# Trunk kernel with a routed expert layer: expert steps of 1024, slabs of 2048, tokens fetched by an indexed DMA

## What is computed

```python
def swiglu(h, w_gate_up, w_down):
    gt, up = jnp.split(h @ w_gate_up, 2, axis=-1)
    return (jax.nn.silu(gt) * up) @ w_down

def moe_swiglu(h, w_router, w_gate_up, w_down):
    t = h.reshape(-1, dm)
    top_val, top_idx = lax.top_k((t @ w_router).astype(jnp.float32), TOP_K)
    top_w = jax.nn.softmax(top_val, axis=-1)
    combine = jnp.sum(jax.nn.one_hot(top_idx, N_EXPERTS) * top_w[..., None], axis=1)
    y = jnp.zeros_like(t)
    for e in range(N_EXPERTS):
        y = y + combine[:, e:e + 1] * swiglu(t, w_gate_up[e], w_down[e])
```

## Time and profile before

| what | value |
|---|---|
| median of 3 runs | 1815.71 us (1814.45 to 1817.58) |
| profiled execution, span from first to last instruction | 1814.0 us |
| expert loop: first matmul of slot 0 | at 793.56 us |
| one slot, steady | 126.2 us, 575 matmul records |
| PE busy over the span | 1770.4 us (98%) |
| DVE, ACT busy over the span | 1375.4 us (76%), 1179.4 us (65%) |
| DMA over one slot | 349 GB/s |

### The profile page before, as it was taken

The page is one execution under the profiler, slowest core; times in us unless marked ns, Lnnn a source line. Parts: engine busy times, 40 slices in busy tenths (PEclk is TensorE's granted clock), DMA queues, the critical chain, the costliest instruction groups (busy, mean ns, idle before and its releaser), DMA issues.

```text
span 1814.0 us, 25521 instructions
## 1 busy us (share of the span) xinstructions
PE 1770.4 (98%) x8224; PEld 1431.1 (79%) x8224; DVE 1375.4 (76%) x1336; ACT 1179.4 (65%) x1313; POOL 79.9 (4%) x108
## 2 busy tenths in 40 slices
PE   7999999999999999889999999999999999999998
PEld 5777877888887778668888888888888888888886
DVE  5654665555665566578998998989989988989987
ACT  5557454434555655357777777777777778777775
POOL 4210000000112100000000000000000000000000
PEclk9999999999999999979999999999999999999999
DMA  8544545656564444749999999999999999999991
GB/s 269 163 142 136 172 142 177 188 182 192 167 196 140 145 149 152 276 174 348 370 335 351 358 342 347 351 345 356 337 349 364 334 353 361 334 356 362 335 352 66
DMA packets 214408, 479.15 MB, mean 264 GB/s; under 512 B 18224, under 2 KB 20304, under 8 KB 214352
## 3 DMA queue, kind: packets, MB, share of 16 engines
q1 hardware_dynamic: 212640, 474.18, 75.6%
q0 software_dynamic: 1712, 4.24, 0.8%
HBM read 477.31 MB, written 1.05 MB: 264 GB/s over the span
## 4 chain that ended last, share of the span: by engine, by line
PE 92%; DVE 4%; ACT 1%; POOL 1%; issue 1%; DMA 0%; DVEq 0%; POOLq 0%; ACTq 0%
PE pa L1663 22%; PE pa L1664 22%; PE pa L1665 22%; PE ps L1663 6%; PE ps L1765 6%; PE ps L1665 6%; PE ps L1664 6%; PE pa L2045 1%; POOL hrs L642 1%; PE ps L1627 1%; DVE w_lo L1094 1%; PE ps L1759 0%; ACT scr L964 0%; DMA gain<-in_mem_norm_g 0%; DVE xt L1130 0%
## 5 line engine op out<-in xcount | busy, mean ns | idle before, releaser
L1663 PE MATMUL pa<-w_hi,r 128*128 128x512 f32 x1496 | 601.4, 402 | 3.0 <-DVE w_lo L1552 3.0
L1665 PE MATMUL pa<-w_hi,r 128*128 128x512 f32 x1496 | 591.3, 395 | 0.0
L1664 PE MATMUL pa<-w_lo,r 128*128 128x512 f32 x1496 | 591.0, 395 | 0.0
L1094 DVE TENSOR_TENSOR w_lo<-w_raw,w_hi 128x1024 fp32r<-128x1024 f32 (+2 forms) x229 | 277.5, 1227 | 140.7 <-ACT w_hi L746 132.9
L746 ACT ACTIVATE w_hi<-w_raw 128x1024 fp32r<-128x1024 f32 (+2 forms) x229 | 237.3, 1050 | 178.6 <-PE pa L1665 154.4
L1663 PEld LDWEIGHTS pa<-w_hi,r 128*128 128x128 f32 x1496 | 281.7, 188 | 69.2 <-DVE w_lo L1552 3.2
L1665 PEld LDWEIGHTS pa<-w_hi,r 128*128 128x128 f32 x1496 | 281.4, 188 | 67.0
L1664 PEld LDWEIGHTS pa<-w_lo,r 128*128 128x128 f32 x1496 | 281.9, 188 | 62.8
L1552 DVE TENSOR_TENSOR w_lo<-w_raw,w_hi 128x1024 fp32r<-128x1024 f32 x160 | 192.3, 1223 | 19.5 <-ACT w_hi L1032 17.1
L1032 ACT ACTIVATE w_hi<-w_raw 128x1024 fp32r<-128x1024 f32 x160 | 167.9, 1060 | 37.9 <-PE pa L1665 21.7
L1663 PE MATMUL ps<-w_hi,r 128*128 128x512 f32 x448 | 177.7, 397 | 0.0
(11 more groups left out here) (261 smaller groups left out, 2041.9 us busy)
## 6 DMA issues: line engine op xcount, KB each, us to landing
w_raw<-in_w_in SPq DMA_DIRECT2D x104, 512.0 KB, 4.3
w_raw<-in_moe_w_gate_up SPq DMA_DIRECT2D x96, 512.0 KB, 5.2
scr<-in_moe_w_gate_up SPq DMA_DIRECT2D x88, 512.0 KB, 5.3
w_raw<-in_moe_w_down SPq DMA_DIRECT2D x64, 512.0 KB, 5.1
w_raw<-in_ff_w_gate_up SPq DMA_DIRECT2D x44, 512.0 KB, 4.5
gates<-in_moe_w_down SPq DMA_DIRECT2D x40, 512.0 KB, 5.1
scr<-in_moe_w_down SPq DMA_DIRECT2D x40, 512.0 KB, 4.8
gr<-in_moe_w_gate_up SPq DMA_DIRECT2D x32, 512.0 KB, 5.4
```

Of the source, the lines that this page charges most:

```text
L1094: dve.tensor_tensor(w_lo[:, s % SPLIT, 0:w], raw_slot(s)[:, 0:w], w_hi[:, s % SPLIT, 0:w].bitcast(F32), ALU.subtract)\
L1663: pe.matmul(dst, hi, m_hi, start=first, stop=False)
L1664: pe.matmul(dst, hi, m_lo, start=False, stop=False)
L1665: return pe.matmul(dst, lo, m_hi, start=False, stop=last)
```

## The change

All SBUF tiles of the trunk and of the expert part are laid out anew, so that the expert part has large tiles of its own over the trunk's. In the expert part:

- Steps are 1024, 1024, 1024 and 512 hidden columns wide, so there are 4 in place of 7.
- A slab is 128 x 2048 (1 MB, 12 matmuls), so a slot has 42 in place of 84. There are 14 raw places in place of 21, and a ring of 3 split slabs in place of 4, with 2 splits ahead of each block in place of 3.
- ACT copies the turned hidden columns first and takes the silu second, since there is now one tile `hs` for both.
- The tokens of slots 1 and on are no longer gathered by `sel`. Two matmuls with two columns (`find_tokens`) give each place its token's number, DVE writes it as an integer (`token_of`), POOL fetches the rows from a copy of the tokens in DRAM (`h_rows`) by an indexed DMA into `xg_tok`, and PE turns them in 8 transposes. `xg` is split by ACT and DVE after that.
- For slot 0 the tokens are gathered by 16 matmuls in plain float32 in place of 32 in fp32r.
- Slot 0 stands outside the loop. It has no scatter, and DVE makes most of the slot tables inside it (`slot_tables`), after its first gate block. Two splits of ACT and DVE come ahead of the gather.

The raw places lie over tiles of the trunk. Eight of the 14 can be loaded at once after the last merge (13 of 21 before); two more wait for the trunk's last split, one for the last norm, two for the router's matmuls, and one for the first gather and the copy of the tokens to DRAM.

```diff
-EXP_RAW, EXP_SPLIT = 21, 4
-EXP_AHEAD = EXP_SPLIT - 1
+EXP_SLAB = 2048
+EXP_RAW, EXP_RING = 14, 3
+EXP_AHEAD = EXP_RING - 1
...
-STEPS = D_EXP // BW
-HT = BW // P
-GU = KT * BW // SLAB
-EXP_SLABS = STEPS * (2 * GU + HT)
-assert EXP_SLABS % EXP_RAW == 0 and EXP_SLABS % EXP_SPLIT == 0
+STEP = [(c, min(DM, D_EXP - c)) for c in range(0, D_EXP, DM)]
+STEPS = len(STEP)
+GU = [KT * w // EXP_SLAB for _, w in STEP]
+DN = [w // P * DM // EXP_SLAB for _, w in STEP]
+EXP_SLABS = sum(2 * a + b for a, b in zip(GU, DN))
+HT = DM // P
+HT_END = STEP[-1][1] // P
+assert EXP_SLABS % EXP_RAW == 0 and EXP_SLABS % EXP_RING == 0
...
+        exp_raw_a = sb("exp_raw_a", [P, 10, EXP_SLAB])
+        hs = sb("hs", [P, DM])
+        exp_hi = sb("exp_hi", [P, EXP_RING, EXP_SLAB], F32R)
+        exp_lo = sb("exp_lo", [P, EXP_RING, EXP_SLAB], F32R)
+        sb("under_gain", [P, DM])
+        exp_raw_b = sb("exp_raw_b", [P, 4, EXP_SLAB])
...
+        exp_slots = [exp_raw_a[:, n, :] for n in range(7)] + [exp_raw_b[:, 3, :]] \
+            + [exp_raw_a[:, n, :] for n in (8, 9, 7)] + [exp_raw_b[:, n, :] for n in (1, 2, 0)]
+        W_RAW_SLOT, GATES_SLOT, XT_SLOT, HN_SLOT = 8, 10, 11, 13
...
+                    if j == XT_SLOT:
+                        sp.wait_ge(slab_used, PRE)
+                    if j == HN_SLOT:
+                        sp.wait_ge(gathered, 1)
+                        sp.wait_ge(h_stored, 16)
+                    dst = exp_slots[j % EXP_RAW].rearrange("p (k n) -> p k n", k=n)
+                    sp.dma_start(dst, src).then_inc(more_ready[j % EXP_RAW], 16)
...
+            pool.wait_ge(norm_done, NT * 3 * LAYERS)
+            pool.dma_start(h_rows[:, :].rearrange("(t p) d -> p t d", p=P), hn[:, :, :])\
+                .then_inc(h_stored, 16)
+            pool.wait_ge(h_stored, 16)
+            def fetch_tokens(i):
+                pool.wait_ge(token_ready, i + 1)
+                pool.sem_inc(token_seen, 1)
+                pool.indirect_dma_start(
+                    out=xg_tok[:, :], out_offset=None, in_=h_rows[:, :],
+                    in_offset=bass.IndirectOffsetOnAxis(ap=token_of[:, 0:1], axis=0),
+                    bounds_check=SEQ - 1, oob_is_err=False).then_inc(token_loaded, 16)
+            fetch_tokens(0)
+            pool.wait_ge(r_table, 1)
+            slots = pool.value_load(slot_i[0:1, 0:1], min_val=EXPERTS, max_val=SLOTS)
+            with pool.Fori(1, slots) as i:
+                fetch_tokens(i)
...
+                def silu(s):
+                    w = STEP[s][1]
+                    act.wait_ge(slab_used, at + (PRE + used))
+                    act.activation(hs[:, 0:w], pa[:, 0:w], ACT.Silu).then_inc(e_silu, 1)
+                def hidden_hi(s):
+                    act.wait_ge(e_turned, i * STEPS + (s + 1))
+                    dst, src = (hts, ps[:, DM:2 * DM]) if s < STEPS - 1 else \
+                        (hts_end, pa[:, BW:2 * BW])
+                    act.activation(dst[:, 0, :, :].rearrange("p k c -> p (k c)"), src, ACT.Copy)\
+                        .then_inc(e_hi, 1)
+                if type(i) is not int:
+                    expert_split(i, EXP_AHEAD)
+                    act.wait_ge(slab_used, at + PRE)
+                    act.activation(ysp[:, 0, :], ps[:, 0:DM], ACT.Copy).then_inc(y_hi, 1)
+                for s in range(STEPS):
+                    uses(GU[s])
+                    if s > 0:
+                        hidden_hi(s - 1)
+                    silu(s)
+                    uses(GU[s])
+                    if s == 0:
+                        act.wait_ge(selt_turned, i + 1)
+                        act.activation(selT[:, :], ps[:, DM:DM + SEQ], ACT.Copy)\
+                            .then_inc(selt_ready, 1)
+                    elif s < STEPS - 1:
+                        uses(DN[s - 1])
+                uses(DN[STEPS - 2] // 2)
+                tokens_hi(i + 2)
+                hidden_hi(STEPS - 1)
+                uses(DN[STEPS - 2] // 2)
+                uses(DN[STEPS - 1])
+                j = 0
...
+            expert_split(0, 1)
...
+            expert_split(0, EXP_AHEAD)
+            def tokens_lo(n):
+                dve.wait_ge(xg_hi, n)
+                dve.tensor_tensor(xg[:, 1, :, :].rearrange("p k c -> p (k c)"), ps[:, DM:2 * DM],
+                                  xg[:, 0, :, :].rearrange("p k c -> p (k c)").bitcast(F32),
+                                  ALU.subtract).then_inc(xg_lo, 1)
+            tokens_lo(1)
...
+            def slot_tables():
+                dve.sem_inc(added, NT)
+                link(dve.memset(ozero, 0.0))
+                link(dve.memset(slot_comb, 0.0))
...
+                if type(i) is not int:
+                    expert_split(i, EXP_AHEAD)
+                    output_lo(i)
+                for s in range(STEPS):
+                    uses(GU[s])
                     if s > 0:
+                        hidden_lo(s - 1)
+                    elif type(i) is int:
+                        slot_tables()
                     else:
                         add_slot(i)
+                    uses(GU[s])
+                    hidden(s)
+                    if s == 0:
                         dve.wait_ge(selt_turned, i + 1)
                         for t in range(NT):
                             dve.tensor_scalar(sel[:, t, :], iota_c[:, :],
                                               slot_pos[:, t, bass.ds(i + 1, 1)], None,
                                               ALU.is_equal).then_inc(sel_ready, 1)
+                    elif s == 1:
+                        dve.wait_ge(token_found, i + 1)
+                        dve.tensor_copy(token_of[:, :], ps[:, DM:DM + 1]).then_inc(token_ready, 1)
+                    if 0 < s < STEPS - 1:
+                        uses(DN[s - 1])
+                uses(DN[STEPS - 2] // 2)
+                tokens_lo(i + 2)
+                hidden_lo(STEPS - 1)
+                uses(DN[STEPS - 2] // 2)
+                uses(DN[STEPS - 1])
+                j = 0
+            expert(0)
...
+            def find_tokens(n):
+                pe.wait_ge(sel_ready, (n + 1) * NT)
+                for t in range(NT):
+                    ins = mm(ps[:, DM:DM + 2], sel[:, t, :], token_no[:, t, :], t == 0, t == NT - 1)
+                ins.then_inc(token_found, 1)
...
+            pe.wait_ge(sel_ready, NT)
+            for k in range(KT):
+                for t in range(NT):
+                    ins = mm(ps[:, DM + k * P:DM + (k + 1) * P], hn[:, t, k * P:(k + 1) * P],
+                             sel[:, t, :], k % 4 == 0 and t == 0, t == NT - 1)
+            ins.then_inc(gathered, 1)
...
+                pe.wait_ge(xg_hi, i + 1)
+                pe.wait_ge(xg_lo, i + 1)
+                for s in range(STEPS):
+                    if s > 0:
+                        pe.wait_ge(e_silu, i * STEPS + s)
+                    block(0, s)
+                    if s > 0:
+                        if s == 1:
+                            pe.wait_ge(selt_ready, i + 1)
+                        elif s == 2:
+                            pe.wait_ge(token_ready, i + 1)
+                        turn_hidden(s - 1)
+                    elif type(i) is not int:
+                        scatter(i)
+                    block(1, s)
+                    if s == 0:
+                        if type(i) is not int:
+                            pe.wait_ge(added, i * NT + NT)
+                        for t in range(NT):
+                            ins = pe.transpose(ps[:, DM + t * P:DM + (t + 1) * P], sel[:, t, :],
+                                               ident[:, :])
+                        ins.then_inc(selt_turned, 1)
+                    elif s < STEPS - 1:
+                        if s == 1:
+                            pe.wait_ge(e_lo, i * STEPS + 1)
+                            find_tokens(i + 1)
+                        down(s - 1, range(DN[s - 1]))
+                half = DN[STEPS - 2] // 2
+                down(STEPS - 2, range(half))
+                pe.wait_ge(token_loaded, i * 16 + 16)
+                for k in range(KT):
+                    ins = pe.transpose(ps[:, DM + k * P:DM + (k + 1) * P],
+                                       xg_tok[:, k * P:(k + 1) * P], ident[:, :])
+                ins.then_inc(gathered, 1)
+                turn_hidden(STEPS - 1)
+                down(STEPS - 2, range(half, 2 * half))
+                down(STEPS - 1, range(DN[STEPS - 1]))
```

More of the change, by code:

```diff
@@ L1006, in _, with expert_split @@
             act.wait_ge(slab_used, PRE)
-            for t in range(NT):
-                act.activation(th[:, 0, t, :], hn[:, t, :], ACT.Copy).then_inc(r_hi, 1)
+            j = 0
+            def expert_split(i, n):
+                nonlocal j
+                while j < min(n, EXP_SLABS):
+                    act.wait_ge(more_ready[j % EXP_RAW], i * (16 * EXP_SLABS // EXP_RAW)
+                                + 16 * (j // EXP_RAW + 1))
+                    act.wait_ge(slab_used, i * EXP_SLABS + (PRE + j - EXP_RING + 1))
```

(31 more changed lines are left out.)

442 lines of the change are left out of this document (172 added, 270 removed).

## The result

| what | before | after |
|---|---|---|
| median | 1816.45 us (1814.45 to 1817.58, 4 runs) | 1785.91 us (1785.56 to 1788.15, 4 runs) |
| ratio | 1 | 0.9835, 95% interval 0.9821 to 0.9849 |
| span of the profiled execution | 1814.0 us | 1784.0 us |
| one slot, steady | 126.23 us | 123.67 us (forecast 125.9) |

The changed kernel is 1.65% faster. The forecast was 1814.4 us with a range of 1803 to 1824, so it was wrong by 28.5 us, and the time lies outside the range.

What follows compares the result with a forecast made beforehand. PE, busy 98% and never waiting in the expert loop, was taken as the bound. Terms -17.3 - 1.8 + 14.8 - 0.7 + 3.7 = -1.3 us gave a span of 1812.7 and a median of 1814.4 us, range 1803 to 1824.

Steps and rivals of the forecast that it cites:

- the first line of the sum: PE's work in a slot: 504 matmuls stay, at 0.2333 us each, 117.6 of the slot's 126.2 us.
- PE's list: PE's instructions in a slot: half gathers go, token transposes and find_tokens come, net -2.16 us a slot, -17.3 for 8.
- Waits at the gate blocks' ends: Steps 1, 2, 3: PE waits 0.76, 0.76 and 0.33 us for the next split, +14.8 us for 8 slots.
- the chain: Gate block's end: ACT's copy, silu and split, then DVE's split, ready at T + 7.47; PE needs it at T + 6.71.
- Split lengths: Splits of 2048 columns, extrapolated from smaller ones: ACT 1.91 us, DVE 2.33 us.
- Near places: Three places elsewhere in a slot where the split chain keeps only 0.1 to 0.2 us of slack; costed at nothing.
- Tables: Slot 0: 25 small DVE instructions, 5.2 us, between the splits of slabs 5 and 6 make PE wait, +3.7 us.
- Start: Before slot 0: first gather from 783.1, 7.4 us as before, PE starts slot 0 at 792.9 for 793.56, -0.7 us.
- Loads: Weights and tokens of a slot need 354 GB/s, where queued slabs move 389 GB/s: zero cost.
- the rival that they bound the slot: Loads or fetch hold PE up: at 349 GB/s a slot takes 127.7 us, the kernel 1828.8 us; chance 0.04.
- the estimate of 124.5 us: Lowest possible slot if a core's HBM share were the skill's 358 GB/s: 44.56/358; the trace's 389 spoke against it.
- the waits don't show: Rival: waits at the gate block's end vanish or show little, the 14.8 falls away, kernel at 1799.6 us; chance 0.31.

Runs made afterwards that it cites:

- gap 1664: Kernel after with 1664 bytes left free ahead of hn, xt0 and r1 (in the expert part exp_raw_b, xg, hts): 1814.47 us, ratio 0.9985.
- Slots without waits: Kernel after with a second silu tile, silu first on ACT: 1770.0 us (slot 121.47); kernel before with tiles placed as after: 1784.09 us (slot 123.29).
- splits cut short: Kernel after with ACT's and DVE's splits in slots 1 to 7 cut from 2048 to 64 columns, products not the reference's: 1765.71 us.

## Why the prediction was wrong, step by step

**The step that failed** is the first line of the sum: "504 matmuls ... stay", at 0.2333 us each. They stayed in number, but their price was taken from a trace with another layout. That the layout was new stood in the change and was given no line, no bound and no rival. It is worth 1784.1 - 1816.2 = -32 us on the kernel before and 1785.9 - 1814.5 = -29 on the kernel after, 1.6 to 1.8%, more than any other term. The trace of before held a hint: alternating distances of 0.229 and 0.237 us for matmuls of one shape at one clock, which suggests that something other than the columns set the pace. I read their mean and went on.

**The rest of the sum holds, in part by luck.** The kernel after at the old pace, with its gap of 1664 bytes, is what was forecast: 1814.5 us against 1814.4, a slot of 125.78 against 125.9. The waits come out nearly as forecast (14.5 against 14.8, 3.6 against 3.7). But PE's list gave 2.7 us less than forecast and the clock behind the tables took 2.5 us that the sum does not have; that the two are not seen is owed to a pace of 0.2324 and not 0.2332 in that run, 504 x 8 x 0.0008 = 3.2 us.

- *PE's list*: -2.16 a slot forecast. Slots without waits, at the same pace, give 121.47 - 123.29 = -1.82. `find_tokens` took 0.36 (forecast 0.44), and the matmul behind it is followed 0.1 late, as are those behind transposes.

```profile
955.94 0.50 PE L1831 MATMUL ps<-token_no,sel 128*128 128x2 f32 x4
956.30 0.49 PE L1729 MATMUL ps<-exp_hi,hts 128*128 128x512 f32 x1
956.63 0.40 PE L1730 MATMUL ps<-exp_lo,hts 128*128 128x512 f32 x1
```

- *Waits at the gate blocks' ends*: three a slot, +14.8 forecast, counted from start to start. So counted they are 17.3 at the new pace (13.5 in the view) and 14.5 at the old one (gap 1664), where the view has 12.4 + 1.3 - 3.2 = 10.5:

```profile
PE pa L1731 <- DVE exp_lo L1523: 12.4, 17, 3.2
PE ps L1731 <- DVE exp_lo L1523: 1.3, 8, 0.2
```

 At the old pace the chain is right to 0.3 us in 14.8. The difference of 2.8 us is the price of speed: a faster PE reaches the late split sooner. This is why the layout gives 32 us before and 29 after, and why, at the new pace, the change's own part is nothing or a small loss (0.9835 against 0.9827, intervals that overlap).

- *Split lengths*: 1.92 and 2.29 us (1.91 and 2.33 forecast). *Near places*: none opened, as costed.
- *Tables*: DVE from 793.78 to 798.72; PE waited 3.4 in the view and 3.6 from start to start (3.7 forecast). The clock behind it, 1.5 us here and up to 2.8, is in no line of the sum.
- *Start*: the forecast had 9.8 us from the first gather to slot 0's first matmul; it took 8.3, since the gather's 32 records took 5.86 us and not 7.4. The granted clock, 0.50 all through the gather of the kernel before, rose in it:

```profile
772.78:776.00 3.22, 3.22 (x15) 3.22 (x16) 2.31 (x2) 0.00 (x0) 0.00 (x0) 0.50 0.24 90
776.00:779.00 3.00, 2.64 (x19) 2.45 (x18) 0.00 (x0) 0.32 (x1) 0.00 (x0) 0.82 0.00 0
```

- *Loads*: the rival that they bound the slot is refuted. The loop ran at 361 GB/s, without waits at 367, and at 376 with splits cut short, and in the kernel after ACT waited for PE alone from 800 us on, never for a transfer. The Trainium skill, DMA: Bandwidth & Descriptors, Specifications, has about 358 GB/s for a core, which it works out as half of what a stack of memory gives two cores. The slots of 123.67, 121.47 and 120.89 us are shorter than the estimate of 124.5 us by that figure, so for a core that runs alone, as here, it is no bound.

Of the rivals none came true. By the direction of the time alone one would pick "the waits don't show" (1799.6), and that would be a false reading: the waits are all there.

## What to carry to other kernels

When a change moves tiles, price the matmuls anew. For 512-column fp32r matmuls as these, keep each stationary tile a multiple of 256 bytes from every moving tile that is read in turn with it; whether it holds for other types no run here shows. It costs a pad of under 256 bytes, and a test is one declaration long. When code that was left alone runs faster in the profile of after, look there first, since the cause is likely something that both parts share. And before a wait is accepted, look at the order of two instructions on the engine that feeds it: here a second tile of 4 KB removed the three in every slot.
